# Mixers of the second block around its attention, and the second tile of expert slots with its own sums and tokens

## The reference

```python
def chunk(xc):                      # 128 tokens at a time
    q = (xc @ w_query).reshape(PEER_CHUNK, PEER_HEADS, 2, half)
    s = jnp.einsum('thpk,pnk->thpn', q, sub_keys)
    sv, si = lax.top_k(s, PEER_TOPK)
    ...
    u = expert_down[eidx]           # 8 heads x 16 picks = 128 rows per token
    vv = expert_up[eidx]
    act = jax.nn.gelu(jnp.einsum('td,thkd->thk', xc, u), approximate=False)
    return jnp.einsum('thk,thkd->td', g * act, vv)
```

```python
attn = attend_query_blocks(q, jnp.concatenate([kc, k], axis=1), ...)
four = fourier_mixer(p[..., OFF_F:OFF_C], w_f)             # real part of fft2, then w_f
conv = conv_module(p[..., OFF_C:OFF_P], ...)               # GLU, 31 taps, layer norm, SiLU, w_pw
pool = pool_mixer(p[..., OFF_P:], w_pl, pl_scale)          # means over 2, 4, 8, 16 tokens, w_pl
x = x + gate1 * (jnp.concatenate([attn, four, conv, pool], axis=-1) @ w_o)
x = x + gate2 * swiglu(xn, w_fi, w_fo)
```

## Time and profile before

| | |
|---|---|
| median of three executions | 2747.05 us (2746.8, 2747.05, 2753.61) |
| profiled execution | 2750.41 us |
| span of its trace | 2748.4 us |
| mean granted TensorE clock | 0.97 |
| PE busy | 2519.2 us, 92% |
| DVE, ACT, POOL busy | 1465.7, 911.2, 610.5 us |
| DMA | 817.45 MB, of it 549.29 MB gathered rows |

### The profile page before, as it was taken

The page is one execution under the profiler, slowest core; times in us unless marked ns, Lnnn a source line. Parts: engine busy times, 40 slices in busy tenths (PEclk is TensorE's granted clock), DMA queues, the critical chain, the costliest instruction groups (busy, mean ns, idle before and its releaser), DMA issues.

```text
span 2748.4 us, 29312 instructions
## 1 busy us (share of the span) xinstructions
PE 2519.2 (92%) x9800; PEld 1714.8 (62%) x9800; DVE 1465.7 (53%) x3160; ACT 911.2 (33%) x2253; POOL 610.5 (22%) x660
## 2 busy tenths in 40 slices
PE   7899999987988989998998989999887999989999
PEld 6568655533444546677555555566355888868888
DVE  1733676888777536414877776777655200162000
ACT  2342354435544322432444445432434200132000
POOL 0000233333343310001333332323316000070000
PEclk9999999999999999999999999999998999989999
DMA  6475999999999974567999999999951444423444
GB/s 254 155 259 183 390 415 427 425 391 380 393 427 427 427 300 167 199 230 282 414 426 426 427 427 388 424 426 427 426 221 62 140 153 152 169 77 123 153 153 153
DMA packets 113645, 817.45 MB, mean 297 GB/s; under 512 B 12432, under 2 KB 14528, under 8 KB 14944
## 3 DMA queue, kind: packets, MB, share of 16 engines
q0 software_dynamic: 75136, 549.29, 47.9%
q1 hardware_dynamic: 38368, 266.35, 26.0%
HBM read 814.54 MB, written 1.05 MB: 297 GB/s over the span
## 4 chain that ended last, share of the span: by engine, by line
PE 61%; DMA 17%; DVE 9%; POOL 5%; issue 5%; ACT 3%; ACTq 0%; DVEq 0%; SPq 0%; POOLq 0%
PE work L652 43%; PE acc L652 17%; DMA arena<-experts,arena 17%; DVE arena L1864 3%; POOL mod_row L641 2%; POOL arena L642 2%; ACT L1397 1%; POOL arena L617 1%; DVE small L1684 1%; DVE arena L1772 1%; PE work L740 1%; DVE arena L1684 1%; ACT arena L1407 0%; DVE arena L1817 0%; ACT arena L1399 0%
## 5 line engine op out<-in xcount | busy, mean ns | idle before, releaser
L652 PE MATMUL acc<-arena 128*128 128x512 f32 (+1 forms) x1900 | 904.6, 628 | 145.6 <-ACT arena L1407 127.6
L1864 DVE SCALAR_TENSOR_TENSOR arena<-arena,acc 128x1024 f32<-128x1024 f32 x512 | 619.4, 1220 | 358.5 <-DMA arena<-experts,arena 325.1
L652 PE MATMUL work<-arena,ring 128*128 128x256 f32 (+2 forms) x3524 | 766.6, 379 | 7.3 <-DVE arena L2046 2.1
L652 PEld LDWEIGHTS work<-arena,ring 128*128 128x128 f32 x3524 | 666.7, 191 | 110.5 <-issue 13.1
L652 PEld LDWEIGHTS acc<-arena 128*128 128x128 f32 (+1 forms) x1900 | 365.6, 199 | 582.5 <-issue 385.5
L617 POOL DMA_INDIRECT arena<-experts,arena x512 | 488.3, 954 | 966.3 <-PE acc L652 833.0
L652 PE MATMUL work<-h,ring 128*128 128x256 f32 (+1 forms) x1440 | 326.1, 380 | 8.2 <-DMA ring<-stream 3.8
L652 PEld LDWEIGHTS work<-h,ring 128*128 128x128 f32 x1440 | 268.4, 192 | 72.5 <-issue 33.7
L1397 ACT ACTIVATE arena<-arena 128x2 f32<-128x2 f32 x256 | 52.0, 203 | 628.4 <-DVE arena L1864 409.5
L652 PE MATMUL work<-lent,ring 128*128 128x256 f32 x992 | 224.2, 379 | 0.0
L652 PEld LDWEIGHTS work<-lent,ring 128*128 128x128 f32 x992 | 188.4, 190 | 52.1 <-issue 29.6
(11 more groups left out here) (257 smaller groups left out, 1812.9 us busy)
## 6 DMA issues: line engine op xcount, KB each, us to landing
ring<-stream SPq DMA_DIRECT2D x252, 1024.0 KB
arena<-experts,arena POOLq DMA_INDIRECT x512
arena<-na_bias POOLq DMA_DIRECT2D x2, 2048.0 KB, 13.7
arena<-consts POOLq DMA_DIRECT2D x1, 2304.0 KB, 17.4
lent<-consts POOLq DMA_DIRECT2D x2, 1024.0 KB, 11.2
arena<-consts POOLq DMA_DIRECT2D x1, 1816.0 KB
x<-x_in SPq DMA_DIRECT2D x1, 1024.0 KB, 5.5
xc<-ctx_in POOLq DMA_DIRECT2D x1, 1024.0 KB, 11.0
```

The costliest lines, as they stand in the source:

```text
L652: ins = nc.tensor.matmul(o, w, r, start=start, stop=stop, **kw)
L1864: ins = v.scalar_tensor_tensor(row, row, 1.0, tok, ALU.mult, ALU.mult, accum_out=dot[:, n:n + 1])
```

## The change

Three things are changed.

1. **The second block's mixers.** POOL only adds: the 30 products of its taps are made by ACT (Identity with a scale, `tap_products`) into a ring of 22 buffers in `hid`, which the feed-forward uses later. ACT puts 18 of them between the copies of the features (`TAPS_BEFORE`), 10 behind these, and the last two behind the first token group. DVE makes all of its 31 taps ahead of the rotation (22 and 9). On PE the first Fourier step and the pooling stand ahead of attention (`MIX_BEFORE`), and the second Fourier step, mean, Fourier product, variance and pooling product at the empty places G0 and G1 within it (`MIX_BETWEEN`). ACT's and DVE's part of them goes into their lists between the pairs of attention. DVE now copies the variance out of PSUM, and ACT takes the root of that copy in place. Behind attention only the pointwise product and the output projection are left.
2. **The second tile.** The sums of the second tile have their own half of `acc` (the half in which the first tile's tokens were). The second tile's tokens are turned at group 21 of the first tile (`second_rows`, two items `rows`) and copied by ACT into the first 128 columns of `h1`, so the dots of the second tile read them from SBUF. ACT copies the first tile's sums in two pieces in groups 65 and 66, behind the weights of these groups, PE turns them at slot 8 of the second tile (`UP_AT`), and DVE adds them at group 70. In the second layer PE adds `y_side` at slot 2 of the second tile (`SIDE_AT`).
3. **Context probability.** ACT's copy of a turned probability (`turned`) stands ahead of the Exp of the same beat.

```diff
+UP_AT = 8
+SIDE_AT = 2
...
-TAPS_FIRST, TAPS_NEXT = 14, 7
-TAPS_PAIR = -(-(CONV - TAPS_FIRST - TAPS_NEXT) // 4)
+TAPS_FIRST = 22
+
+TAPS_BEFORE = {4: 3, 5: 4, 6: 4, 7: 4, 8: 3}
+TAPS_THEN = 10
+
+MIX_BEFORE = ("dft", "dft", "pool", "pool")
+MIX_BETWEEN = {("G0", 0): ("dft",), ("G0", 1): ("mean",), ("G1", 1): ("four", "four"), ("G0", 2): ("var",),
+               ("G1", 2): ("plin", "plin")}
...
+            if q == ROWS_AT:
+                add(f"rows{l}", 2)
+            if q == TILE_GROUPS + UP_AT // GROUP:
                 add(f"ytr{l}", 2)
...
-        y_acc = acc[:, 0:D]
-        tok = acc[:, D:2 * D]
+        y_acc = [acc[:, t * D:(t + 1) * D] for t in range(TT)]
+        tok = [acc[:, D:2 * D].rearrange("p (k t) -> p k t", t=P), h1[:, :, 0:P]]
...
-                    src = glu[:, 1, j:j + T]
...
-                        G.step(nc.gpsimd.tensor_scalar(tap_p, src, w[:, j:j + 1], None, ALU.mult))
-                        G.step(nc.gpsimd.tensor_tensor(o, o, tap_p, ALU.add),
-                               "conv_pool" if j == CONV - 1 else None)
+                        G.need("tap_made", l * (CONV - 1) + j)
+                        G.step(nc.gpsimd.tensor_tensor(o, o, hid[:, (j - 1) % KF, :], ALU.add), "tap_added")
...
+                def second_rows():
+
+                    for a in range(2):
+                        b = bank(f"rows{l}", a)
...
+                            transpose_to(b[:, i * P:(i + 1) * P], h1[:, 4 * a + i, P:2 * P], k1("ident"),
+                                         bank_full if i == 3 else None)
...
-                        mm(y_acc[:, a * 512:(a + 1) * 512], diag[:, at_diag % DIAGS, :], up[:, s, a * 512:(a + 1) * 512],
+                        mm(y_acc[t][:, a * 512:(a + 1) * 512], diag[:, at_diag % DIAGS, :], up[:, s, a * 512:(a + 1) * 512],
...
                 context = context_rest() if l else context_mixers()
                 for t in range(TT):
                     if t:
...
+                        pe.wait_ge(sem(f"dotted{l}"), TILE_GROUPS)
                     for j in range(SLOTS):
...
+                        if l and t and j == SIDE_AT:
+                            add_side(t - 1)
+                        if t and j == UP_AT:
+                            for a in range(2):
+                                add_up(t - 1, a)
...
+                            if n // GROUP == ROWS_AT:
+                                second_rows()
...
+                def mix_between(kind, p):
+                    if (kind, p) == ("G0", 0):
+                        dn = k2("dft_n")
+                        b = bank(f"dft{l}", 2)
...
+                    elif (kind, p) == ("G0", 1):
+                        b = bank(f"mean{l}")
+                        pe.wait_ge(sem("conv"), l + 1)
+                        pe.wait_ge(sem("tap_added"), (l + 1) * CONV)
...
+                    elif (kind, p) == ("G1", 1):
+                        copied(pe, f"dft{l}", 2)
+                        for n in range(2):
...
+                    elif (kind, p) == ("G0", 2):
+                        b = bank(f"var{l}")
+                        pe.wait_ge(sem("csq"), 2 * l + 2)
...
+                            if u >= 2:
+                                turned(u - 2)
                             A.need("score_c", u + 1)
                             c = prob_c[u % 3]
                             A.step(f(c, c, ACT.Exp, bias=neg_mx[:, u % 3, 0:1], accum_out=total[:, u % 3, 0:1]), "exp_c")
-                            if u >= 2:
-                                turned(u - 2)
...
+                def sums_out(t, a):
+                    if l:
+                        A.need(f"summed{l}", t + 1)
+                    else:
+                        m = l * PICKS + (t + 1) * SLOTS - 1
+                        act.wait_ge(rows_free[m % ROWS], m // ROWS + 1)
+                    o = slice(a * 512, (a + 1) * 512)
+                    A.step(f(y_row[:, o], y_acc[t][:, o], ACT.Copy), f"y_row{l}")
...
+                    if q - 1 == ROWS_AT:
+                        for a in range(2):
+                            b = A.full(f"rows{l}", a)
+                            A.free(f(tok[1][:, 4 * a:4 * a + 4, :], b[:, :].rearrange("p (k t) -> p k t", t=P), ACT.Copy),
+                                   f"rows{l}", a)
+                    if q in (TILE_GROUPS + SIDE_AT // GROUP, TILE_GROUPS + SIDE_AT // GROUP + 1):
+                        sums_out(0, q - TILE_GROUPS - SIDE_AT // GROUP)
...
+                        if j > KF:
+                            A.need("tap_added", l * CONV + j - KF + 1)
+                        A.step(f(hid[:, (j - 1) % KF, :], glu[:, 1, j:j + T], ACT.Identity, scale=w[:, j:j + 1]),
+                               "tap_made", last=False)
+                        yield
...
+                    for _ in range(TAPS_BEFORE.get(i, 0)):
+                        next(products)
...
+                for _ in range(TAPS_THEN):
+                    next(products)
...
+                def mix_after_exp(u):
+                    if u == 2:
+                        b = A.full(f"dft{l}", 2)
+                        A.free(f(flat(yf[:, :, :]), b[:, :], ACT.Copy), f"dft{l}", 2)
...
+                def mix_after_turn(p):
+                    if p == 1:
+                        copied(act, f"mean{l}", 0)
+                        for g in range(2):
+                            A.step(f(csq[:, g, :], cv[:, g, :], ACT.Square), "csq")
...
+                    elif p == 2:
+                        copied(act, f"var{l}", 0)
+                        A.step(f(rnorm2, rnorm2, ACT.Sqrt, bias=k1("eps")), "var_root")
+                        for g in range(2):
+                            b = A.full(f"plin{l}", g)
+                            A.free(f(mix[:, 6 + g, :], b[:, 0:T], ACT.Identity, scale=k2("pool_scale", l)[:, g:g + 1]),
+                                   f"plin{l}", g)
+                    elif p == 3:
...
+                        for g in range(2):
+                            A.need("conv_normed", 2 * l + g + 1)
+                            A.step(f(cs[:, g, :], cv[:, g, :], ACT.Silu, scale=k2("ln_g", l)[:, g:g + 1],
+                                     bias=k2("ln_b", l)[:, g:g + 1]), "cs")
...
+                        for a in range(2):
...
+                        row = down[:, m % ROWS, :].rearrange("p (k t) -> p k t", t=P)
+                        ins = v.scalar_tensor_tensor(row, row, 1.0, tok[t], ALU.mult,
...
+                    if q == TILE_GROUPS + UP_AT // GROUP + 2:
+                        for a in range(2):
+                            add_up(0, a)
...
+                for _ in taps:
+                    pass
...
+                def mix_after_pair(p):
+                    if p == 0:
...
+                    elif p == 1:
+                        b = V.full(f"var{l}")
+                        V.free(v.tensor_copy(rnorm2, b[:, 0:T]), f"var{l}")
...
+                    elif p == 2:
+                        V.need("var_root", l + 1)
+                        V.step(v.reciprocal(rnorm2, rnorm2))
...
+                attention(f"attx{l}", units2(), prob2, mix_after_pair)
```

202 lines of the change are left out of this document (88 added, 114 removed).

## The result

The changed kernel takes **2722.03 us** (median of four, 2721.01 to 2722.75) where the one before took 2750.33 beside it (2746.8 to 2754.94): a ratio of 0.9896, interval 0.9881 to 0.991. It is 28 us faster; 43 were forecast, and 2722 lies above the upper end of the range, 2720. The profiled execution took 2722.66 us, 27.75 less than that of before.

The account below looks back on a forecast made before the run. The gather was taken to bound the expert loops, and PE the second block's feed-forward, with other engines on the chain after attention. 2750.41 - 30.6 (second block) - 7.8 - 4.5 (tile changes) = 2707.5, or 2704 against the median; range 2694 to 2720.

Parts of the forecast that it names:

- The tail, the term of 9.8 us: Second block, third pair's probability copy to output projection: 9.8 us instead of 27.0, four pointwise matmuls at 1.8.
- Taps: Second block: DVE's 31 taps at 0.625 us beside POOL end before PE has rotated, 2082.0 against 2083.6.
- One of the prediction's own signs of being wrong: Second block, ahead of attention: DVE's taps ending after PE has rotated would show the forecast wrong.
- The layers repeat one another: Second block: both layers have the same timing, so 15.3 us gained per layer makes 30.6.
- Attention: Second block: with mixers put in, the third pair's probabilities are copied at 2108.5 instead of 2106.6, 1.9 us late.
- attention stretches: Rival, second block: inserted work does not hide or DVE's taps end late, 9 us gained a layer, 2717; chance 0.12.
- First tile change, 7.8 us: First layer's expert loop, first to second token tile: 7.8 us gained of 12.8 lost there, range 3 to 12.8.
- bank order: Rival, expert loops: the wait moves from tokens to slot 138, so loops give only 2 us, 2714; chance 0.20.
- Second tile change, 4.5 us: Second layer's expert loop, first to second token tile: dots start 5.87 us earlier, 4.5 gained, range 0 to 6.1.
- only bytes not moved lengthen the loop: Expert loops: the gather bounds them at 427 GB/s, losing 12.8 and 6.1 us behind the tile changes.
- The slower rival: Second tiles: each gather instruction holds up one dot, DVE becomes the bound, 2788 us; chance 0.03.
- a wait longer than 5 us at a later output: First layer's second tile: PE waiting longer than 5 us at slot 138 would show the forecast wrong; about 4.3 expected.

Follow-up runs that it names:

- after_again: The changed kernel run once more, unaltered, on the chip of the following runs: 2719.66 us, ratio 0.989.
- fill_tail: Changed kernel plus nine unread matmuls per layer in PE's waits between the third pair's turned probabilities and the pointwise product: 2718.94 us, ratio 0.9892.
- after: The changed kernel itself, with all three parts of the change: 2722.03 us, ratio 0.9896 against the kernel before.
- pool_behind: Changed kernel in which POOL begins its additions only behind DVE's seventeenth tap: 2718.1 us, ratio 0.9896.
- probability_after: Changed kernel with part 3 undone, ACT's copy of the turned context probability behind the Exp again: first layer's slots 128 to 160 take 83.4 us.
- block_only: Kernel before with only part 1 of the change, the second block's mixers: 2724.35 us, ratio 0.9915.
- dots_sbuf_both: Changed kernel in which the first tile's dots also read tokens from SBUF, from group 26 on: 2719.22 us in a single execution.
- gap_again: Changed kernel in which PE waits at slot 128 for two more groups of dots: expert loops 698.0 us in the first layer, 737.1 in the second.
- sums_slot12: Changed kernel with the first tile's sums turned at slot 12 of the second tile instead of 8: 2723.4 us in a single execution.

## Why the prediction was wrong

The waits that it named are gone or smaller. But the gains were put too high, and above all two steps failed: the price of PE's work behind short waits, and the account of the second loop. 42.9 us were forecast against the profiled execution, 27.75 came. Of the 15.2 missing, 8 are in the second block (22.6 of 30.6, of which 1.2 came unforeseen, from a higher clock ahead of the first tap that after_again doesn't have) and 7 in the loops and the stage between them.

- **The tail, the term of 9.8 us.** Its order and its ScalarE part were right: the pointwise product begins 7.3 us behind the copy, 7.6 by my sum. The step that failed priced the four matmuls at 0.45 us each, the rate of the earlier trace rows on a PE that had been busy. Here PE stands 0.89, 1.14 and 1.30 us in turn for ScalarE just before:

```profile
2103.63 1.09 PE L666 MATMUL work<-arena 128*64 128x128 f32 x16 [0.89 <-ACT arena L1353]
2105.87 1.16 PE L754 MATMUL work<-c,arena 128*128 128x128 f32 x8 [1.14 <-ACT arena L1719]
2108.33 1.98 PE L666 MATMUL work<-arena 128*64 128x128 f32 x16 [1.30 <-ACT arena L1353]
```

  The trace of before had shown what follows such waits (the 1.94 of the earlier trace rows against about 1.1 for the same turn later), and I used it for the first pair and not for the last. It cost 1.8 us in each layer and 1.9 at the second layer's output projection, 5.5 in this trace; fill_tail shows that it is the clock. In after_again the same step costs 2.7.
- **Taps.** 31 x 0.625 was the rate beside POOL's mixture of products and additions. Beside additions alone, each with two inputs, DVE's taps take longer: 35 instructions of this group now have a mean of 716 ns, against 625 in the earlier trace rows, while POOL's addition stays at 781:

```profile
L1754 DVE SCALAR_TENSOR_TENSOR arena<-arena 128x256 f32<-128x256 f32 x35 | 25.0, 716 | 5.7 <-ACT arena L1684 4.5
...
L657 POOL TENSOR_TENSOR arena<-arena 128x256 f32<-128x256 f32 x30 | 23.4, 781 | 4.9 <-ACT arena L1662 2.7
```

  The prediction had named 0.1 us a tap with 1.5 us for it, and took nothing; scores begin 2.85 us later instead of 1.7, 2.3 us in both layers. One of the prediction's own signs of being wrong came with it: PE has rotated at 2077.28, DVE's taps end only at 2079.25, and PE then stands 1.11 us for DVE:

```profile
2079.29 0.69 DVE L2187 TENSOR_TENSOR arena<-work,arena 128x512 f32<-128x512 f32 x1
...
2080.12 3.81 PE L666 MATMUL work<-arena 128*128 128x256 f32 x16 [1.11 <-DVE arena L2187]
```

  That the whole of the 2.3 is the taps isn't shown, since undoing most of the slowdown gave nothing back.
- **The layers repeat one another:** not the tail before, which was 26.96 in the first layer and 25.85 in the second; 1.1 us.
- **Attention:** the third copy 0.3 us later, 0.2 by the sum. The rival "attention stretches" did not come.
- **First tile change, 7.8 us:** 8.1 in the two traces (88.5 to 80.4), 7.3 to 8.9 in the kernels with slot 8. The reading of the windows was right. What the loop gave back: 1.5 behind the change, 0.9 ahead of it, and 2.4 in its first 24 slots. So the rival "bank order" did not come, though both loops together gave 4.5 us of the 12.3, which is nearer to its 2.
- **Those 24 slots** take 70.4 to 72.3 us or 74.1 to 75.2, also among kernels with the same instructions up to there (after and pool_behind). The slow ones have a low clock as the last queries are made; first after, then probability_after:

```profile
270.00:280.00 10.00, 9.20 (x48) 7.57 (x52) 9.42 (x31) 0.77 (x2) 2.87 (x4) 0.66 0.00 0
```

```profile
270.00:280.00 10.00, 7.98 (x61) 5.10 (x61) 9.40 (x31) 1.36 (x3) 2.95 (x4) 1.00 0.13 31
```

  Whether the change makes the slow start likelier (seven of eleven kernels with its loops, none of the two without them) stays open.
- **Second tile change, 4.5 us:** 3.7 in the two traces (123.4 to 119.7; block_only, with the loops of before, has 122.0), but the whole loop gained only 1.2. In every kernel with the second part the 87 slots behind it take 250.4 to 251.6 us, against 248.3 and 249.3. The windows of these slots, before and after:

```profile
1758.63:2006.91 248.28, 229.63 (x766) 144.54 (x765) 179.68 (x353) 86.24 (x241) 85.06 (x87) 0.97 1.01 426
```

```profile
1751.28:2001.70 250.42, 229.99 (x766) 144.50 (x765) 179.74 (x353) 86.21 (x241) 96.97 (x87) 0.97 1.01 424
```

  424 GB/s for 426 is 1.2 of these 2.1 us; the rest went to 0.4 MB more in the same slots. The loop as a whole, from its first gather to its last, moves 310.6 MB instead of 310.0 by the trace's DMA packets (310.3 to 310.7 in all eleven kernels with the second part, 309.9 in block_only), and 0.6 MB are 1.3 us at 427 GB/s: half of the 2.5 us that the loop gave back. Which of the change's edits does it isn't settled: the longer gathers (11.9 us more of POOL) are excluded by the first tiles of dots_sbuf_both as far as these resemble the second, and gap_again speaks against the loop simply swallowing a gap. The failed step is "only bytes not moved lengthen the loop": it was applied to the stretch at the change and not to the rest, and it took the bytes between the first and the last gather as given.
- **The slower rival** (dots held up by gathers) was wrong by its direction: the gather waits for the dot, 0.18 us per row as a mean, beside idle time of POOL. Of the prediction's other signs of being wrong, a wait longer than 5 us at a later output did not come, but sums_slot12 shows how near it was.

By the Trainium skill (SBUF — State Buffer, "Who interferes with whom") VectorE and GpSimd lock the port pair that they share. The trace agrees for taps beside additions (16.3 us for 21 against 12.1), and for the gather's instruction, which ends 0.81 us behind the dot; here the loss is GpSimd's (0.94 to 1.13 us) and hardly VectorE's (1220 to 1225 ns).

## What to carry to other kernels

Price work behind a string of short waits at the clock that such a place had in the trace, not at the rate of a busy stretch; and where PE's waits can't be removed, a few matmuls that nobody reads may pay (3.6 us in the tails of two layers and 1.9 behind them against the trace of after, about half of that against after_again). When banks are handed round in the order of a list, moving one item moves the bank of each item behind it: four slots' difference was a wait of 2.18 or 8.71 us. A stall that goes is counted over the whole loop, with the bytes that the loop moves: here 3.7 us at the spot were 1.2 at the end.

## What was not expected of the hardware

The granted clock fell to 0.51 in the 10 us behind a stretch in which PE was busy 6.68 of 10, and stayed at 1.00 with 9.46. A gather instruction of POOL took 1.13 us as a mean beside dots that read both inputs from SBUF and 0.94 beside dots that read one from PSUM, while the dots' median moved only from 1220 to 1225 ns; nearly all of the long ones (80 of 91) ended 0.80 to 0.82 us behind a DVE instruction of 1024 columns with both inputs in SBUF.
